# Seven quarter products instead of eight in both feed-forward products, in two passes with the activations kept in memory between them

## The chip, the cores and the metric

The kernel runs on one core of a Trainium2 chip. The metric is the device time in microseconds of one execution, given as the median of several runs. Changes under 0.3% of it are not told from none here.

## The reference

One layer of a streaming encoder for 1024 frames of width 1024, all in float32. A mixer part (three kinds of attention and recurrence, computed in `front` and `heads`) ends in `mixed @ w_out`. What the change touches comes behind it:

```python
x = x + rmsnorm(mixed, post_mix_g[l])
h = rmsnorm(x, pre_ffn_g[l])
ff = jnp.square(jax.nn.relu(h @ w_ff1[l])) @ w_ff2[l]     # w_ff1: 1024 x 4096, w_ff2: 4096 x 1024
x = x + rmsnorm(ff, post_ffn_g[l])
```

## The kernel before

Every large product is computed in three passes: an operand is cut into a high part (a copy rounded to the matmul's type, `fp32r`) and a low part (operand minus high part), and low x high, high x low and high x high are added up in one bank of PSUM. So each operand needs one copy, mostly on ScalarE, and one subtraction, mostly on VectorE, before TensorE can use it.

The function `back` holds all that is changed. It is written as one program for each engine (SyncE issues the loads and stores, ScalarE, GpSimd, VectorE, TensorE), and the programs meet at semaphores; each engine takes its instructions in the order written. It starts with the output projection (`product(j, half)`, L1648), takes rows j of 128 frames through `residual(j)` and the normalising (`rows`, `normed_rows`), and turns them with eight transposes each (`turn(j)`, L2051) into `hH` and `hL`, the transposed activations (1024 of depth in 8 blocks, 1024 frames).

The feed-forward part runs over 8 slices of 512 hidden columns (`NE`), each in 4 blocks (`FB`) of 128. `hidden_half` (L2058) makes a block of hidden columns for 512 frames: 8 blocks of depth x 3 passes = 24 matmuls of 128x512. `second_product` (L2081) multiplies a slice with its 512 rows of `w_ff2`: 16 groups (8 tiles of frames x 2 halves of columns) of 4 x 3 = 12 matmuls. On ScalarE a hidden block goes through ReLU (L1864) and square (L1867); VectorE cuts it (L1975, L1977) into `gH` and `gL`. Weights are loaded by SyncE (L1742, L1747), copied on ScalarE (L1809, L1815) and subtracted on VectorE (L1906, L1910). The sum over slices is kept in SBUF, in `acc`, 128 x 8192: VectorE adds each group's bank to it (L1987), 128 times; GpSimd sets it to zero (L1893). Slices 0 to 6 are one loop (`Fori`) on each engine:

```python
with pe.Fori(0, NE - 1) as e:
    hidden_block(e + 1, 0)
    second_product(e)
    for i in range(1, FB):
        hidden_block(e + 1, i)
second_product(NE - 1)
```

`finish(j)` normalises the rows of `acc` while the last slice still runs; behind the last matmul come an add, a square with its sum (L1883), a root, two scaled halves (L2008), two adds (L2011) and two stores (L1794).

`front` uses GpSimd and VectorE at once, and the rows below take durations from it: GpSimd subtracts 128x256 pieces (L484) while VectorE works on 128x768 tiles (L919, L927, L931).

## Time and profile before

| | |
|---|---|
| median of 3 runs | 1529.02 us (1528.37 to 1533.39) |
| span of the profiled execution, first to last instruction | 1526.5 us |
| feed-forward part, first to last matmul | 807.48 to 1517.70 us |
| TensorE busy | 1445.1 us, 95% |
| VectorE, ScalarE, GpSimd busy | 679.8, 536.7, 308.4 us |
| moved by DMA | 124.15 MB, mean 81 GB/s |

The profiled execution has no device time of its own beside the span; the median lies 2.5 us over the span. Times of rows are microseconds from the first instruction unless marked ns. PE is TensorE's matmul, PEld its weight load, DVE VectorE, ACT ScalarE, POOL GpSimd. Matmuls overlap, and the durations in their rows hold the overlap; the distance of their starts tells their pace.

### The profile page before, as it was taken

The page shows a single profiled execution, that of the slowest core. Times are in us where ns is not written, and L with a number is a line of the kernel's source. Part 1 is how long each engine was busy: PE and PEld are TensorE (multiplying, and loading weights), DVE is VectorE, ACT ScalarE, POOL GpSimd, SP SyncE. Part 2 cuts the span into 40 slices and gives each one's busy share as a digit, 9 for nine tenths or more (in the row PEclk, how much of TensorE's full clock was granted, in tenths as well). Part 3 has the DMA queues.
Part 4 walks back from the last instruction along what each step waited for, and adds up shares of the span by engine and source line. Part 5 has one row for each costly group of instructions (what it writes and reads, how often), then busy time and mean ns, then how long its engine had stood idle before and what let it go on. Part 6 is the DMA issues. An engine that isn't in the chain of part 4 may idle for free.

```text
span 1526.5 us, 27877 instructions
## 1 busy us (share of the span) xinstructions
PE 1445.1 (95%) x11404; PEld 1135.9 (74%) x11404; DVE 679.8 (45%) x1101; ACT 536.7 (35%) x1045; POOL 308.4 (20%) x423
## 2 busy tenths in 40 slices
PE   6999989989898999889999999999999999999997
PEld 5887677777676666465777888888888888888876
DVE  6244252556554375755555233242423324242347
ACT  4533231434323588875434213030211304031222
POOL 6674635423240142433001000000000000000000
PEclk9999999999999799999999999999999999999999
DMA  6554423423234603021623203020110302021024
GB/s 192 146 157 126 133 57 104 120 60 99 59 78 95 177 3 84 3 88 54 204 102 119 70 10 101 0 87 22 56 54 14 96 0 96 14 69 41 27 67 168
DMA packets 144429, 124.15 MB, mean 81 GB/s; under 512 B 31437, under 2 KB 122762, under 8 KB 144330
## 3 DMA queue, kind: packets, MB, share of 16 engines
q1 hardware_dynamic: 98044, 92.90, 20.0%
q10 hardware_dynamic: 46286, 29.84, 7.0%
q8 instruction: 73, 1.20, 0.3%
q14 instruction: 26, 0.21, 0.0%
HBM read 97.88 MB, written 24.84 MB: 80 GB/s over the span
## 4 chain that ended last, share of the span: by engine, by line
PE 48%; DVE 2%; ACT 1%; DMA 1%; issue 1%; POOLq 0%; SPq 0%; DVEq 0%; ACTq 0%
PE all_ps_b L2081 23%; PE all_ps_b L2058 22%; PE all_ps_b L1648 2%; DMA bk_acc<-in_w_out 1%; POOLq L1668 0%; DVE bk_acc L1935 0%; PE all_ps_b L2051 0%; ACT bk_acc L1836 0%; DVE bk_acc L1945 0%; DVE bk_w1L L1906 0%; DVE bk_acc L1931 0%; DVE all_hL L1951 0%; DVE all_gL L1977 0%; ACT bk_rect L1867 0%; DVE bk_acc L2008 0%
## 5 line engine op out<-in xcount | busy, mean ns | idle before, releaser
L1987 DVE TENSOR_TENSOR bk_acc<-bk_acc,all_ps_b 128x512 f32<-128x512 f32 x128 | 88.0, 687 | 275.9 <-PE all_ps_b L2081 275.8
L2058 PE MATMUL all_ps_b<-all_hH,bk_w1L 128*128 128x512 f32 x512 | 200.1, 391 | 5.1 <-PE all_ps_b L2081 2.2
L2081 PE MATMUL all_ps_b<-bk_w2H,all_gL 128*128 128x512 f32 x512 | 200.0, 391 | 2.5 <-DVE all_gL L1977 2.5
L2081 PE MATMUL all_ps_b<-bk_w2H,all_gH 128*128 128x512 f32 x512 | 199.8, 390 | 0.0
L2081 PE MATMUL all_ps_b<-bk_w2L,all_gH 128*128 128x512 f32 x512 | 199.7, 390 | 0.0
L2058 PE MATMUL all_ps_b<-all_hH,bk_w1H 128*128 128x512 f32 x512 | 199.3, 389 | 0.0
L2058 PE MATMUL all_ps_b<-all_hL,bk_w1H 128*128 128x512 f32 x512 | 199.2, 389 | 0.0
L484 POOL TENSOR_TENSOR fr_wL<-fr_raw,fr_wH 128x256 fp32r<-128x256 f32 (+1 forms) x208 | 162.7, 814 | 78.0 <-PE fr_ps_F L1259 54.5
L1259 PE MATMUL fr_ps_F<-fr_hL,fr_wH 128*128 128x512 f32 (+1 forms) x416 | 168.1, 404 | 2.6 <-DVE fr_hL L803 2.1
L1259 PE MATMUL fr_ps_F<-fr_hH,fr_wH 128*128 128x512 f32 (+1 forms) x416 | 166.1, 399 | 0.0
L1815 ACT CAST bk_w2H<-all_raw 128x1024 fp32r<-128x1024 f32 x32 | 32.9, 1047 | 355.6 <-PEq L2086 351.7
L2058 PEld LDWEIGHTS all_ps_b<-all_hH,bk_w1L 128*128 128x128 f32 x512 | 96.1, 188 | 28.3 <-issue 6.8
L2081 PEld LDWEIGHTS all_ps_b<-bk_w2H,all_gL 128*128 128x128 f32 x512 | 96.5, 188 | 23.0 <-DVE all_gL L1977 2.9
L1259 PE MATMUL fr_ps_F<-fr_hH,fr_wL 128*128 128x512 f32 (+1 forms) x416 | 112.4, 400 | 0.0
L2081 PEld LDWEIGHTS all_ps_b<-bk_w2H,all_gH 128*128 128x128 f32 x512 | 96.5, 188 | 20.2
L2081 PEld LDWEIGHTS all_ps_b<-bk_w2L,all_gH 128*128 128x128 f32 x512 | 96.5, 189 | 19.9
L2058 PEld LDWEIGHTS all_ps_b<-all_hH,bk_w1H 128*128 128x128 f32 x512 | 96.1, 188 | 20.1
L2058 PEld LDWEIGHTS all_ps_b<-all_hL,bk_w1H 128*128 128x128 f32 x512 | 96.1, 188 | 19.5
L1259 PEld LDWEIGHTS fr_ps_F<-fr_hL,fr_wH 128*128 128x128 f32 (+1 forms) x416 | 76.8, 185 | 22.4 <-issue 3.8
L1975 DVE CAST all_gH<-bk_rect 128x512 fp32r<-128x512 f32 x64 | 27.3, 427 | 145.9 <-ACT bk_rect L1867 145.9
L1259 PEld LDWEIGHTS fr_ps_F<-fr_hH,fr_wH 128*128 128x128 f32 (+1 forms) x416 | 76.9, 185 | 18.6 <-issue 2.0
L1259 PEld LDWEIGHTS fr_ps_F<-fr_hH,fr_wL 128*128 128x128 f32 (+1 forms) x416 | 75.6, 185 | 19.8 <-issue 3.2
(354 smaller groups left out, 2260.9 us busy)
## 6 DMA issues: line engine op xcount, KB each, us to landing
fr_raw<-in_w_in ACTq DMA_DIRECT2D x37, 512.0 KB, 4.2
bk_raw<-in_w_ff SPq DMA_DIRECT2D x32, 512.0 KB, 4.3
all_raw<-in_w_ff SPq DMA_DIRECT2D x32, 512.0 KB, 4.7
projected<-fr_stage ACTq DMA_DIRECT2D x39, 256.0 KB, 4.4
fr_raw<-in_w_in SPq DMA_DIRECT2D x13, 512.0 KB, 4.2
fr_xt<-in_x SPq DMA_DIRECT2D x8, 512.0 KB, 4.9
bk_acc<-in_x SPq DMA_DIRECT2D x8, 512.0 KB, 3.4
x_after_mixers<-bk_acc SPq DMA_DIRECT2D x8, 512.0 KB, 2.6
```

The costliest lines, as they stand in the source:

```text
L484: m = pool.tensor_tensor(wL[b][:, k:k + 2, 0:wd], raw[b][:, k:k + 2, 0:wd], wH[b][:, k:k + 2, 0:wd].bitcast(F32), ALU.subtract)
L1259: m = pe.matmul(F[b][0:wd, :], w[b][:, k, 0:wd], a[:, k, :], start=(at_ == 0), stop=(at_ == len(passes) - 1))
L1648: i = pe.matmul(bank[:], m[:, k, ts], w[:, k, :], start=(k == first and q == 0), stop=(k == last and q == 2), skip_group_check=True)
L1815: act.copy(w2H[:, i, :], raw2[i % 2][:]).then_inc(w2_high, 1)
L1975: dve.tensor_copy(gH[:, i, hs], g32).then_inc(g_high, 1)
L1987: dve.tensor_tensor(acc[:, j, ds], acc[:, j, ds], ybank[g % 4][:], ALU.add).then_inc(collected, 1)
L2058: m = pe.matmul(bank[s][h][:], w[s][:, k, :], a[:, k, hs], start=(k == 0 and q == 0), stop=(k == KB - 1 and q == 2))
L2081: m = pe.matmul(ybank[g % 4][:], a[:, i, ts], w[:, i, ds], start=(i == 0 and q == 0), stop=(i == FB - 1 and q == 2))
```

## The change

Both products are split into quarters, one level of Strassen's scheme in the form with seven products and shared sums. In the first one the hidden columns are taken in 16 pairs p of blocks (block p and block 16 + p), and the depth and the frames are halved. For each pair there are seven products P1 to P7 of 4 blocks of depth x 3 passes = 12 matmuls (`hidden(q)`, in the order `SEQ`; the first pairs' P1 and P2 are drawn ahead). GpSimd makes four sums of weight quarters for each pair, and GpSimd and VectorE make four sums of activation quarters once, tile by tile as they are turned. VectorE adds the products up (`drain`), rectifies and squares three quarters of the result, ScalarE the fourth (`take_c11`), and SyncE stores all to a new tensor in memory, `rectified`, 4096 x 1024.

The second product starts when the first is done. It runs over s = 0, 1, 2 (two of the seven products each: M3 and the one beside it, M1 and M2, M7 and M4) and k = 0 to 15 (128 hidden columns of either half each): 2 products x 4 tiles of frames x 3 passes = 24 matmuls for each k, added up over k in eight banks. The seventh product (`last_product`) is added behind them, tile by tile; for k under 12 (`KEPT`) its operands are prepared in s = 2 and kept in SBUF. Each quarter is loaded again for each s (`load_unit`; the two quarters of s = 0 stay for s = 1) into nine slots; `POOL_SUMS` and `DVE_SUMS` are added on GpSimd and VectorE; ScalarE copies the high parts, VectorE subtracts the low parts, into a ring `R` of four products. Between the s VectorE and ScalarE take the banks out and combine them (`take_tiles`, `tile_sum`). `acc`, its memset and the 128 adds are gone; nothing of the part is a loop any more.

The core of the diff:

```diff
--- before.py
+++ after.py
@@ -1656,40 +1656,225 @@
...
+        SEQ = [(0, P1), (1, P1), (0, P2), (1, P2), (2, P1), (2, P2)]
+        for p in range(3):
+            SEQ += [(p, i) for i in (P6, P5, P7, P4, P3)]
+        for p in range(3, NP):
+            SEQ += [(p, i) for i in (P1, P6, P2, P5, P7, P4, P3)]
+        NQ, AT = len(SEQ), {x: q for q, x in enumerate(SEQ)}
...
+        KEPT = 12
...
+            pairs_ = {0: [("b12", "b22")], 1: [("a22", "b11"), ("b22", "b21")],
+                      2: [("a21", "a22"), ("b11", "b21")] + ([("a11", "b12")] if k < KEPT else []),
+                      3: [("a21", "a11"), ("b11", "b12")]}[s]
+            UNITS += [(s, k, names) for names in pairs_]
...
+        def products(s, k):
+            if s == 0:
+                return [("a11", "b12", 1), ("temp", "b22", -1)]
+            if s == 1:
+                return [("a11", "b11", 1), ("a12", "b21", 1)]
+            if s == 2:
+                return [("a22", "b21", 1), ("a21", "b11", -1)]
+            return [("a11", "b12", 1)]
+        POOL_SUMS = {0: [("b12", "b12", "b22", ALU.subtract), ("temp", "a11", "a12", ALU.add)],
+                     1: [("a11", "a11", "a22", ALU.add), ("b11", "b11", "b22", ALU.add), ("b21", "b21", "b22", ALU.add)],
+                     2: [("a11", "a21", "a11", ALU.subtract), ("a21", "a21", "a22", ALU.add), ("b12", "b11", "b12", ALU.add)],
+                     3: [("a11", "a21", "a11", ALU.subtract)]}
+        DVE_SUMS = {0: [], 1: [("a12", "a12", "a22", ALU.subtract)], 2: [("b21", "b21", "b11", ALU.subtract)],
+                    3: [("b12", "b11", "b12", ALU.add)]}
...
+        def LEAD(q):
+            return min(9 + 2 * (q - EARLY + 1), q + 9)
+        FIRST_F = {NQ - 6: (0,), NQ - 5: (1,), NQ - 3: (2,), NQ - 2: (3,)}
...
+            def load_unit(u):
+                s, k, names = UNITS[u]
+                if u < SLOTS:
+                    sp.wait_ge(made, NQ - SLOTS + u + 1)
+                else:
+                    sp.wait_ge(*split_done(*UNITS[u - SLOTS][0:2]))
...
+            def take_c11(p):
+                m = M[p, 0]
+                c = cbuf[m % 3]
+                act.wait_ge(made, AT[p, P2] + 1)
...
+                act.activation(c, b(p, 1)[:], ACT.Relu).then_inc(c11_taken, 1)
+                act.wait_ge(c11_taken, p + 1)
+                act.activation(c, c, ACT.Square).then_inc(c11_ready, 1)
...
+            t_split(2, 45)
+            residual(TB - 1)
+            take_p1(0)
+            take_high(TB - 2)
+            rows(TB - 1)
+            t_split(3, 45)
+            t_split(4, 45)
+            take_p1(1)
+            split(4)
+            split(5)
+            take_c11(0)
+            for n in (2, 1, 3, 4):
+                t_split(n, 6)
+            take_c11(1)
+            take_high(TB - 1)
+            take_p1(2)
+            t_split(2, 7)
+            t_split(1, 7)
+            split(6)
...
+                    act.wait_ge(*used_at(at - 4))
+                raw_ready(s, k, a)
+                act.copy(R[at % 4][0], place(s, k, a)).then_inc(f_high, 1)
+                raw_ready(s, k, w)
+                if sign < 0:
+                    act.activation(R[at % 4][2], place(s, k, w), ACT.Copy, scale=-1.0).then_inc(f_high, 1)
+                else:
+                    act.copy(R[at % 4][2], place(s, k, w)).then_inc(f_high, 1)
...
+            for p in range(NP):
+                a, w = rawA[p % 3], rawB[p % 2]
+                pool.wait_ge(a_in[p % 3], 16 * (p // 3 + 1))
+                pool.wait_ge(b_in[p % 2], 16 * (p // 2 + 1))
+                if p:
+                    pool.wait_ge(low, max(AT[p - 1, P5], AT[p - 1, P6]) + 1)
+                else:
+                    pool.wait_ge(turned, 2 * TB)
+                pool.tensor_tensor(S1, w[:, LO], w[:, HI], ALU.add).then_inc(ssum, 1)
+                pool.wait_ge(ssum, 4 * p + 1)
+                pool.tensor_tensor(S2, S1, a[:, LO], ALU.subtract).then_inc(ssum, 1)
+                pool.tensor_tensor(w[:, LO], a[:, LO], w[:, LO], ALU.subtract).then_inc(ssum, 1)
+                pool.wait_ge(ssum, 4 * p + 2)
+                if p:
+                    pool.wait_ge(low, AT[p - 1, P3] + 1)
+                pool.tensor_tensor(S4, a[:, HI], S2, ALU.subtract).then_inc(ssum, 1)
+            for s, k in BLOCKS:
+                for n, (to, a, w, op) in enumerate(sums_of(POOL_SUMS, s, k)):
+                    if n == 0:
+                        for u in units_of(s, k):
+                            pool.wait_ge(u_in[unit_slot(u)], IN_COUNT[u])
+                        if s == 1:
+                            pool.wait_ge(*split_done(0, k))
+                    if to == "temp":
+                        if k < 2:
+                            pool.wait_ge(u3_made, NP - 1 + k)
+                        else:
+                            pool.wait_ge(*split_done(0, k - 2))
+                    if (s, to) == (2, "a21") and k < KEPT:
+                        pool.wait_ge(f_sum, POOL_AT[s, k, "a11"])
+                    pool.tensor_tensor(place(s, k, to), place(s, k, a), place(s, k, w), op).then_inc(f_sum, 1)
...
+                if i == P6:
+                    dve.wait_ge(p1_taken, p + 1)
+                    if p:
+                        dve.wait_ge(c12_sum, p)
+                    else:
+                        dve.wait_ge(t_low, len(T_ORDER))
+                    dve.tensor_tensor(u2, p1_of(p), b(p, 2)[:], ALU.add).then_inc(u2_made, 1)
+                if i == P7:
+                    if p:
+                        dve.wait_ge(c21_sum, p)
+                    dve.tensor_tensor(u3, p1_of(p), b(p, 2)[:], ALU.add).then_inc(u3_made, 1)
+                    c = room(p, 3)
+                    dve.wait_ge(u3_made, p + 1)
+                    dve.tensor_tensor(c, u3, b(p, 3)[:], ALU.add).then_inc(c22_sum, 1)
+                    dve.wait_ge(c22_sum, p + 1)
+                    rectify(p, 3)
...
+            for s, k in BLOCKS:
+                add_pieces(s, k)
+                for n in range(len(products(s, k))):
+                    if number(s, k, n) >= 4:
+                        split_product(s, k, n)
+                    if (s, k, n) == (1, 0, 1):
+                        for j in range(4):
+                            dve.wait_ge(m3_taken, j + 1)
+                            tile_sum(j, 5 + j, c12[j], c22[j], bankB[j][:], ALU.subtract, c12_made)
+                    if (s, k, n) == (2, 0, 1):
+                        for j in range(4):
+                            dve.wait_ge(m1_taken, j + 1)
+                            tile_sum(j, 9 + j, c22[j], c22[j], bankA[j][:], ALU.add, m1_added)
+                        for j in range(4):
+                            tile_sum(j, 13 + j, c11[j], c11[j], bankB[j][:], ALU.add, m7_added)
...
+                for k in range(QB):
+                    for n, (w, a) in enumerate(((wL, aH), (wH, aL), (wH, aH))):
+                        m = pe.matmul(bank[:], w[:, k, :], a[:, k, :], start=(begins and k == 0 and n == 0),
+                                      stop=(k == QB - 1 and n == 2), skip_group_check=True)
+                m.then_inc(made, 1)
...
+            def second_product(s, k, n):
+                at = number(s, k, n)
+                pe.wait_ge(f_low, at + 1)
...
+                    if s == 1 and k == 0:
+                        if n:
+                            pe.wait_ge(c12_made, j + 1)
+                        else:
+                            pe.wait_ge(m3_taken, j + 1)
+                    if s == 2 and k == 0:
+                        if n:
+                            pe.wait_ge(m7_added, j + 1)
+                        else:
+                            pe.wait_ge(m1_taken, j + 1)
+                            pe.wait_ge(m1_added, j + 1)
+                    m = tile((bankB if n else bankA)[j], j, R[at % 4], begins, last)
+                    if last:
+                        m.then_inc(tile_done, 1)
+                if not last:
+                    m.then_inc(used, 1)
...
+            def last_product(j, ks):
+                for k in ks:
+                    if k < KEPT:
+                        pe.wait_ge(k_low, 2 * k + 2)
+                        pieces = m6[k]
+                    else:
+                        pe.wait_ge(f_low, number(3, k, 0) + 1)
+                        pieces = R[number(3, k, 0) % 4]
+                    if k == 0:
+                        pe.wait_ge(c21_made, j + 1)
+                    m = tile(bankB[j], j, pieces, False, k == NK - 1)
+                if ks[-1] == NK - 1:
+                    m.then_inc(tile_done, 1)
...
+            hidden(0)
             turn(TB - 2)
-            pe.wait_ge(w1_low[1], 2)
-            hidden_half(1, 0)
+            for q in (1, 2, 3):
+                hidden(q)
             turn(TB - 1)
-            pe.wait_ge(freed, TB)
-            pe.wait_ge(hlow, 2 * TB)
-            hidden_half(0, 1).then_inc(hidden[0], 1)
-            hidden_half(1, 1).then_inc(hidden[1], 1)
-            hidden_block(0, 2)
-            hidden_block(0, 3)
-            with pe.Fori(0, NE - 1) as e:
-                hidden_block(e + 1, 0)
-                second_product(e)
-                for i in range(1, FB):
-                    hidden_block(e + 1, i)
-            second_product(NE - 1)
+            for q in range(4, NQ):
+                hidden(q)
+            for s in range(3):
+                for k in range(NK):
+                    for n in range(2):
+                        second_product(s, k, n)
+            for j in range(2):
+                last_product(j, range(KEPT))
+            for j in range(2):
+                last_product(j, range(KEPT, NK))
+            for j in range(2, 4):
+                last_product(j, range(NK))
...
+    rect_d = nc.dram_tensor("rectified", [DFF, T], F32, kind="Internal").ap()
```

## Rows read from the trace of the kernel before

**Rows 1.** The page, 40 slices of the span: TensorE's busy share and granted clock, in tenths.
```profile
PE   6999989989898999889999999999999999999997
...
PEclk9999999999999799999999999999999999999999
```
**Rows 2.** Stretches of the span: length, busy us (instructions) of PE, PEld, DVE, ACT, POOL, clock, DMA.
```profile
807.48:1517.70 710.22, 702.60 (x3089) 578.57 (x3087) 257.99 (x365) 156.95 (x236) 6.95 (x1) 1.00 0.18 58
1517.70:1526.50 8.80, 0.00 (x0) 0.00 (x0) 3.87 (x8) 1.50 (x5) 0.00 (x0) 0.78 0.31 120
```
**Rows 3.** The page, groups by line: form and count, busy us, mean ns, idle before.
```profile
L1987 DVE TENSOR_TENSOR bk_acc<-bk_acc,all_ps_b 128x512 f32<-128x512 f32 x128 | 88.0, 687 | 275.9 <-PE all_ps_b L2081 275.8
L2058 PE MATMUL all_ps_b<-all_hH,bk_w1L 128*128 128x512 f32 x512 | 200.1, 391 | 5.1 <-PE all_ps_b L2081 2.2
```
**Rows 4.** Timeline of PE inside a loop turn: start, us, instruction; 27 intervals.
```profile
1239.86 0.39 PE L2081 MATMUL all_ps_b<-bk_w2H,all_gH 128*128 128x512 f32 x1
...
1245.98 0.39 PE L2081 MATMUL all_ps_b<-bk_w2H,all_gH 128*128 128x512 f32 x1
```
**Rows 5.** Waits of PE from 800 us on: who for whom, total us, times, longest.
```profile
PE all_ps_b L2081 <- DVE all_gL L1977: 2.5, 1, 2.5
PE all_ps_b L2058 <- PE all_ps_b L2081: 2.2, 7, 0.3
PE all_ps_b L2058 <- DVE all_hL L1951: 1.7, 1, 1.7
PE all_ps_b L2058 <- DVE bk_w1L L1906: 1.3, 1, 1.3
```
**Rows 6.** Timeline of PE: a turn of tiles, a loop turn, behind the last wait.
```profile
819.26 1.04 PE L2051 MATMUL all_ps_b<-all_ident,bk_acc 128*128 128x128 f32 x8
...
910.47 0.39 PE L2081 MATMUL all_ps_b<-bk_w2H,all_gH 128*128 128x512 f32 x1
911.15 0.47 PE L2058 MATMUL all_ps_b<-all_hH,bk_w1L 128*128 128x512 f32 x1 [0.30 <-PE all_ps_b L2081]
...
1475.65 0.63 PE L2081 MATMUL all_ps_b<-bk_w2L,all_gH 128*128 128x512 f32 x1
1476.08 0.63 PE L2081 MATMUL all_ps_b<-bk_w2H,all_gH 128*128 128x512 f32 x1
...
1478.50 0.39 PE L2081 MATMUL all_ps_b<-bk_w2H,all_gH 128*128 128x512 f32 x1
```
**Rows 7.** Groups by line and form, 700 to 800 us: operations of 128x512.
```profile
L1915 DVE TENSOR_TENSOR bk_w2L<-bk_acc,bk_w2H 128x512 fp32r<-128x512 f32 x8 | 5.4, 692 | 14.4 <-ACT bk_w2H L1819 14.4
...
L1843 ACT CAST all_hH<-all_ps_b 128x512 fp32r<-128x512 f32 x10 | 5.3, 583 | 0.1
...
L1819 ACT CAST bk_w2H<-bk_acc 128x512 fp32r<-128x512 f32 x8 | 5.0, 622 | 15.3 <-DMA bk_acc<-in_w_out 15.2
```
**Rows 8.** GpSimd: timeline at 70 to 115 us, then a group by line and form.
```profile
70.00 2.82 POOL L484 TENSOR_TENSOR fr_wL<-fr_raw,fr_wH 128x256 fp32r<-128x256 f32 x4
...
102.93 5.57 POOL L484 TENSOR_TENSOR fr_wL<-fr_raw,fr_wH 128x256 fp32r<-128x256 f32 x4
...
114.36 1.03 POOL L478 CAST fr_wH<-fr_raw 128x1024 fp32r<-128x1024 f32 x1
...
L484 POOL TENSOR_TENSOR fr_wL<-fr_raw,fr_wH 128x32 fp32r<-128x32 f32 x8 | 1.8, 252 | 8.0 <-PE fr_ps_F L1259 8.0
```
**Rows 9.** Timeline of VectorE in the same time.
```profile
101.00 0.96 DVE L919 TENSOR_TENSOR fr_bt<-fr_kk,fr_sa 128x768 f32<-128x768 f32 x1
...
103.59 1.49 DVE L927 SCALAR_TENSOR_TENSOR fr_at<-fr_kk,fr_at 128x768 f32<-128x768 f32 x1
105.00 1.49 DVE L931 SCALAR_TENSOR_TENSOR fr_sw<-fr_sw,fr_ks 128x768 f32<-128x768 f32 x1
...
114.33 0.69 DVE L956 TENSOR_TENSOR fr_bonus<-fr_vs,fr_ps_S 128x512 f32<-128x512 f32 x1 [1.88 <-PE fr_ps_S L1319]
```
**Rows 10.** A stretch: length, PE busy, granted clock, DMA share, GB/s.
```profile
820.00:860.00 40.00, 37.03 (x164) 1.00 0.37 120
```

More of the change, by code:

```diff
@@ L1874, in _ @@
[L1874 to L1886 removed]
+            t_split(1, 45)
@@ new lines, in _, with take_tiles @@
+            for q in range(EARLY, NQ):
+                p, i = SEQ[q]
+                if i == P1:
+                    take_p1(p)
+                if i == P2:
+                    take_c11(p)
+                while next_q < min(NQ, LEAD(q)):
+                    split(next_q)
+                    next_q += 1
+                for n in FIRST_F.get(q, ()):
+                    split_product(0, n // 2, n % 2)
+            def take_tiles(to, bank, after, done):
+                for j in range(4):
+                    act.wait_ge(tile_done, after + j + 1)
+                    act.copy(to[j], bank[j][:]).then_inc(done, 1)
@@ new lines, in _ @@
+            t_split(1, 45)
+            t_split(2, 45)
+            residual(TB - 1)
+            take_low(TB - 2)
+            normed_rows(TB - 1)
+            t_split(3, 45)
+            t_split(4, 45)
+            split(4)
+            split(5)
+            for n in (2, 1, 3, 4):
+                t_split(n, 6)
+            take_low(TB - 1)
+            t_sums()
+            t_split(2, 7)
+            t_split(1, 7)
+            split(6)
+            t_split(3, 7)
+            t_split(4, 7)
+            split(7)
@@ new lines, in split_kept @@
+            def split_kept(k):
+                aH, aL, wH, wL = m6[k]
+                dve.wait_ge(k_high, 2 * k + 1)
+                dve.tensor_tensor(aL, place(2, k, "a11"), f32(aH), ALU.subtract).then_inc(k_low, 1)
+                dve.wait_ge(k_high, 2 * k + 2)
+                dve.tensor_tensor(wL, place(2, k, "b12"), f32(wH), ALU.subtract).then_inc(k_low, 1)
+            for q in range(EARLY, NQ):
+                drain(q)
+                while next_q < min(NQ, LEAD(q)):
+                    split(next_q)
+                    next_q += 1
+                for n in FIRST_F.get(q, ()):
+                    split_product(0, n // 2, n % 2)
```

819 lines of the change are left out of this document (574 added, 245 removed).

## The prediction

> **What bounds the kernel now.** I read the slices of the page first: from the middle of the span on, TensorE shows 9 tenths or more in every slice, and its clock is granted in full nearly throughout [rows 1]. The table of stretches cuts out the two feed-forward products: from the first matmul of L2058 at 807.48 us to the end of the last of L2081 at 1517.70 us, 710.2 us, with TensorE busy 702.6, VectorE 258.0, ScalarE 157.0, GpSimd 7.0; behind it 8.8 us of tail [rows 2]. The groups by line say that this is 3072 matmuls of 128x512, all alike, and that VectorE mostly waits for them (275.9 us before its adds at L1987) [rows 3]. A row gives 0.39 us for a matmul, but they overlap; what one costs is the distance of starts: 27 of them in 1239.86 to 1245.98, 6.12 us, 0.2267 us each [rows 4]. 3072 x 0.2267 = 696.4 us; two groups of eight transposes are 2.1; so 11.7 us are waits. The list of waits and the starts name them: 7 loop turns (0.68 us between the starts across a turn instead of 0.23 and a little more at the next one, some 0.54 each, 3.8 in all), about 3.4 us at the entrance (1.7 and 1.3 and what goes with them), and 4.3 us in the last slice (2.5 of waiting, then about nine matmuls at up to 0.43 instead of 0.23), where there is nothing to fill with [rows 5, 6]. So TensorE is the bound here, and 98% of the stretch is matmuls.
>
> **What goes.** 1536 + 1536 matmuls become 16 x 7 x 4 x 3 = 1344 for the first product (16 pairs of column blocks, 7 products, 4 blocks of depth, 3 passes for high and low parts) and 16 x 7 x 4 x 3 = 1344 for the second. 384 fewer of the same shape: 384 x 0.2267 = **87.1 us**. The code is no longer a loop: 3.8 us less. The last slice's wait and the slow matmuls after it go: 4.3. The two waits at the entrance are replaced by others, counted below: 3.4. The memset of 7 us on GpSimd goes, too; it only lay beside. Sum of what goes: 98.6 us.
>
> **The new entrance.** Six products (first quarter operands only) can run before the sums of quarters of the activations are there: 72 matmuls and two turns, 16.3 + 2.1 us after 807.5, so TensorE is at product seven (P6) at 826. ScalarE has to do in that time, one after the other: two squares with their sums and a root (1.8), take_p1 three times, take_high of tiles 6 and 7 at three copies each, four split copies of 128x512 for tile 6, two for tile 7, three weight splits, two rows of 1024 (the square with its root, and two splits of 1024: 3.5) and c11 twice (2.4). At 0.58 to 0.62 us for a 512-column copy [rows 7] that is about 19 us, starting 0.8 us late behind t_split(2,45). It ends near 827.5; on VectorE come three quarter sums of the last tile (1.9) and the low parts (0.6 each) in the same chain, so P6 starts near 830 to 831. I take 5 us of waiting, 1.5 for the slow clock after it and 1.5 for the first pairs, where VectorE has two splits a product to make up its lead: **8 us**, bounds 0 (all hidden) and 15 (each step also queued behind GpSimd).
>
> **Pass one.** A pair lasts 84 x 0.2267 = 19.0 us. VectorE has 7 splits, 5 adds from PSUM, 3 rectifies: 15 x 0.6 to 0.69, about 10 us; ScalarE 10 operations of 0.6, 6 us; GpSimd 4 sums, 5 us; splits lead by up to nine products. All of it lies beside the matmuls: 0. Between the passes TensorE waits for the last drain of P3, 0.2 + 0.69 plus a semaphore: **1.2 us**. The stores to memory have 0.85 us of issue and some 3 us of flight a block; the first blocks read back after the last product (k = 2, 3) have 11 us until they are due.
>
> **Pass two: where the next bound is.** One k is 24 matmuls, 5.44 us. Per k there are: s=0: 2 GpSimd sums, 4 VectorE operations; s=1: 3 and 5; s=2, k under 12: 3 and 7 (one sum, four low parts, two kept ones); ScalarE 4 to 6 copies, 3.7 us at most. All are 128x512 with both inputs in SBUF. Alone, VectorE takes 0.69 us for one, about 0.61 from start to start [rows 7]. For GpSimd the trace has no 128x512 sum; four of 128x256 take 2.82 us alone, 0.705 each, and one of 128x32 0.25 [rows 8]: 2.0 ns a column, so 1.22 us for 512 (bounds: 0.87 by half that slope, 1.41 by twice the 256-column one). By these s=2 would be 7 x 0.61 = 4.3 us on VectorE and 3 x 1.22 = 3.7 on GpSimd, and both would fit beside 5.44.
>
> But they don't run beside each other. From 102.93 us on the same four GpSimd subtractions take 5.57 us, 1.39 each, exactly while VectorE runs operations with two SBUF inputs, and these, of 768 columns, start every 1.41 us, where one alone takes 0.96 and about 0.87 from start to start [rows 8, 9]. 1.41 for a pair whose parts alone are 0.705 + 0.87 = 1.58: the two engines take turns, at 0.89 of the sum. Where VectorE reads PSUM (0.69 us at 114.33) GpSimd's cast beside it stays at 1.03 [rows 8, 9]. The Trainium skill (GPSIMD Engine Reference, Key points) says that GpSimd shares its SBUF interfaces with VectorE and that instructions with two SBUF inputs contend; by that rule, too, the two columns add up. The same page (Elementwise, side-by-side cycle accounting) has 4497 ns for 2048 columns, so an estimate of 1.12 us for 512; no run here shows that shape, and with it the sum below would be about 5 us less.
>
> So per k: s=0: (4 x 0.61 + 2 x 1.22) x 0.89 = 4.3 us, under 5.44; s=1: (5 x 0.61 + 3 x 1.22) x 0.89 = 6.0; s=2: (7 x 0.61 + 3 x 1.22) x 0.89 = 7.1. TensorE then waits 0.53 us a k in s=1, from about k=4 on, when VectorE's lead of up to four products is eaten: 12 x 0.53 = 6. In s=2 1.62 a k over 11: 18. Between s=1 and s=2 TensorE's first tiles wait for m1_added, which VectorE reaches only behind both splits of k=0 (5 operations and GpSimd's 3 between them, 6 us, against 2.7 of matmuls), and then four m7 adds stand ahead of the next split: 4 + 2 = 6. Sum **30 us**. Between s=0 and s=1 the copy and c12 have 2.7 us of matmuls over them: 0. Behind k=12 of s=2 it is (5 x 0.61 + 1.22) x 0.89 = 3.8, no wait; the last product needs nothing new for 12 of 16 k. Bounds of this term: 0 (the leads and nine load slots cover it) and 60 (bubbles of 1 us a k on top, since sum, copy and low part go over three engines).
>
> DMA: s=2 loads 6 x 256 KB, 1.57 MB a k, 289 GB/s at full pace, 223 at 7.1 us. One stretch of the same queue moved 120 GB/s at a share of 0.37, so full use would be about 324 [rows 10]: it carries it, and I take 0; a share of 0.9 is the closest rival for the blame.
>
> The tail has the same chain as before behind its last matmul (add, square, root, two scaled halves, two stores): 0.
>
> **Sum.** 1526.5 - 98.6 + 8 + 1.2 + 30 = 1467.1 us of span. The median of the runs is 1529.0, 2.5 over this span, and I keep that: **1470 us**.
>
> **The rivals.** (a) The sharing doesn't bite: the load slots let GpSimd run up to four k ahead, and its sums fall into VectorE's pauses. Then 1467 - 30 = 1437, so 1440 us. For it: s=0 has slack, and VectorE stands idle for several us ahead of each block of tile sums. Against: GpSimd takes its turn whenever a slot is free, so its lead is never spent. 25%. (b) The chain over the engines binds on top of the shared reads: sum on VectorE or GpSimd, copy on ScalarE, low part on VectorE, each with 0.1 to 0.3 us between; 1 us more for each of 28 k, 1498 us. 12%. (c) The slower side: the many short waits of s=1 and s=2 bring TensorE's clock to its lower level and keep it there. After the wait of 2.5 us the starts went from 0.23 to 0.43 us for a while (1475.65 to 1476.08), 1.2 GHz in place of 2.4; after the one of 1.7 us at 820 there is no such stretch [rows 5, 6]. At that level a k takes 24 x 0.427 = 10.2 us, against 6.0 and 7.1: over all 28 k 100 us more, 1570 us, slower than before; it decides from about 17 k at that level on. Against it: with 10.2 us a k nobody has to be waited for, the matmuls are dense again, and after the wait at 1471 the clock came back once they were (0.39 us for the matmul at 1478.50, 0.63 for those before) [rows 6]. The Trainium skill (TensorE: Matmul & The Clock Gate, A second HAM failure mode) has a kernel that idles a little between groups of matmuls and swings between the two levels; by that rule some of (c) would come. 6%. That the change doesn't do what it says would show as more than 2688 matmuls; the loops of the diff leave no room for that.
>
> **How the numbers follow.** Forecast 57%, (a) 25, (b) 12, (c) 6. The likeliest's own range is 1453 to 1488. Of the 20% left out at most, (c)'s bulk and the ends of (a) and (b) are part: 1437 to 1500. A difference under 0.3%, 4.6 us, can't be told from none here. (c) in part only could land anywhere between, so slower is 6%, same 1%, faster 93%.
>
> **What would show it.** After: 2688 matmuls of 128x512 in the feed-forward part, 0.2267 us apart in pass one, in a stretch near 310 + 8 us. In pass two, s=0 dense; from s=1 on gaps before products, released by VectorE's splits; VectorE's 128x512 subtractions and GpSimd's sums there well above 0.69 and 1.22 us, VectorE and GpSimd together busy nearly all the time. If the sums stay at 1.22 and TensorE has no gaps, (a) is right. If VectorE idles while TensorE waits, (b), or DMA if the releaser is a landing. I am wrong altogether if pass one has waits on each pair, or if the granted clock is under 0.95 over pass two.

## The result, and the profile after

| | before | after |
|---|---|---|
| median, same chip | 1531.2 us (4 runs) | 1483.49 us (4 runs, 1480.28 to 1488.01) |
| ratio | | 0.9687 (95%: 0.9663 to 0.9710) |
| span; device time of the profiled execution | 1526.5 | 1482.4; 1484.15 us |
| feed-forward part, first matmul to end of last | 710.2 us | 811.04 to 1473.84: 662.8 us |
| TensorE, VectorE, GpSimd busy | 1445.1, 679.8, 308.4 us | 1373.6, 925.7, 610.1 us |
| moved by DMA | 124.15 MB | 185.34 MB |

3.1% faster. The forecast was 1470 us, 13.5 under the result, which lies inside the likeliest case's own range, 1453 to 1488. The measure that I use below is the *excess* of a stretch: its length less 0.2268 us for each of its matmuls, the pitch of [rows 4] taken over the dense stretches. Before, the part had 710.2 - 3072 x 0.2268 = 13.5 us of it; after, 662.8 - 2688 x 0.2268 = 53.2.

The slices of the page after, for TensorE, its clock and VectorE; the second product is the last nine or so. Where [rows 1] had nines, there are now eights, and it is VectorE that has the nines:
```profile
PE   6999989989899899898989799999999999998897
...
DVE  6244162565652465667375985555556989999985
...
PEclk9999999999999799999999999999999999999999
```
The table of stretches, columns as in [rows 2]: the entrance, pass one, then s = 0, s = 1, s = 2 (k under 12, k from 12 on), the last product, the tail:
```profile
807.00:862.00 55.00, 44.73 (x193) 35.66 (x192) 46.97 (x55) 28.86 (x53) 32.43 (x20) 0.94 0.28 88
862.00:1130.90 268.90, 268.90 (x1187) 222.44 (x1186) 146.78 (x216) 78.94 (x137) 77.82 (x56) 1.00 0.37 116
1133.40:1220.30 86.90, 86.90 (x383) 71.93 (x384) 72.37 (x60) 35.91 (x64) 61.32 (x39) 1.00 0.61 215
1220.30:1320.00 99.70, 92.90 (x387) 70.65 (x386) 99.61 (x89) 39.12 (x73) 71.38 (x44) 1.00 0.53 174
1320.00:1402.00 82.00, 67.13 (x265) 50.94 (x266) 81.24 (x83) 34.16 (x64) 49.99 (x32) 0.96 0.61 197
1402.00:1430.00 28.00, 27.29 (x120) 22.12 (x119) 27.74 (x36) 14.77 (x28) 10.49 (x7) 1.00 0.87 291
1430.00:1473.70 43.70, 43.66 (x192) 35.96 (x192) 28.02 (x50) 12.42 (x32) 0.00 (x0) 1.00 0.37 143
1473.70:1482.40 8.70, 0.14 (x1) 0.00 (x0) 3.81 (x7) 0.93 (x3) 0.00 (x0) 0.72 0.16 61
```
Pass one is dense. In s = 1 VectorE is busy 99.6 of 99.7 us, in s = 2 81.2 of 82: it is the bound there, and 1 - 67.13/82 = 18% of TensorE's time is lost. By the starts of the 2688 matmuls the excess is 13.4 us at the entrance (to 854.40), 4.1 in pass one with its end, 0.7 in s = 0, 11.7 in s = 1, 22.1 in s = 2 below k = 12, 0.9 above, 0.1 in the last product: 53.0 (the last matmul's end is the other 0.2). TensorE's waits from 807 us on, who for whom, total, times, longest:
```profile
PE all_ps_b L2661 <- DVE ro_w1A L2492: 10.1, 9, 2.7
PE all_ps_b L2661 <- DVE ro_hH L2492: 8.2, 8, 4.3
PE all_ps_b L2652 <- DVE ro_slot L2336: 7.9, 3, 5.6
PE all_ps_b L2661 <- DVE pl_raw L2466: 2.3, 1, 2.3
PE all_ps_b L2652 <- ACT pl_p L2141: 1.6, 1, 1.6
...
PE all_ps_b L2652 <- ACT pl_raw L2141: 0.8, 1, 0.8
```
The first four are VectorE: two rows for the low parts of the second product, one for the entrance, one for the border of the passes. The two of ScalarE are its copies of P1 out of PSUM at the entrance. No landing releases TensorE. For VectorE the list of waits has no row in s = 1 and in s = 2 below k = 12, while GpSimd waits 41.2 us for landings there: a late sum of GpSimd is not what holds VectorE up.

The timelines of VectorE (first fence) and GpSimd (second) around the largest gap of the second product, and TensorE's rows there (third):
```profile
1334.37 0.68 DVE L2499 TENSOR_TENSOR ro_gL<-pl_slot,ro_gL 128x512 fp32r<-128x512 f32 x1
1334.97 1.77 DVE L2480 TENSOR_TENSOR pl_slot<-pl_slot 128x512 f32<-128x512 f32 x1
1336.67 1.78 DVE L2487 TENSOR_TENSOR ro_w1A<-pl_slot,ro_w1A 128x512 fp32r<-128x512 f32 x1
...
1346.86 1.74 DVE L2480 TENSOR_TENSOR pl_slot<-pl_slot 128x512 f32<-128x512 f32 x1
```
```profile
1334.44 5.16 POOL L2329 TENSOR_TENSOR pl_slot<-pl_slot 128x512 f32<-128x512 f32 x3 [9.31 <-DMA pl_slot<-in_w_ff]
...
1344.65 1.73 POOL L2329 TENSOR_TENSOR pl_slot<-pl_hT,pl_slot 128x512 f32<-128x512 f32 x1
```
```profile
1344.65 2.01 PE L2661 MATMUL all_ps_b<-ro_xt 128*128 128x512 f32 x8
1350.94 2.62 PE L2661 MATMUL all_ps_b<-ro_hH 128*128 128x512 f32 x6 [4.28 <-DVE ro_hH L2492]
```
The operation before 1334.97, with GpSimd idle, lasts 0.68 us and the next starts 0.60 after it. From there eight in a row start 1.70 us apart (1334.97 to 1346.86 is 7 x 1.70): as soon as GpSimd has work, the engines alternate, one instruction each. GpSimd's sums beside VectorE (first row) and alone (second), from the entrance of the same trace:
```profile
830.99 1.74 POOL L2313 TENSOR_TENSOR all_sb_masks<-pl_w1A,pl_y 128x512 f32<-128x512 f32 x1
840.84 1.28 POOL L2306 TENSOR_TENSOR pl_y<-pl_xt 128x512 f32<-128x512 f32 x1 [8.11 <-DVE ro_slot L2336]
```
So a pair takes 1.70 us where the parts alone are 0.60 + 1.28 = 1.88: 0.90 of the sum. Over all of s = 1, 41 of VectorE's 81 such operations last over 1.5 us, for 42 GpSimd sums; in s = 2 below k = 12 it is 30 of 83, for 32 sums. **Each GpSimd sum lengthens one VectorE operation by 1.10 us.** Behind the 4.3 us wait about nine matmuls follow at the lower level of the clock (starts 0.43 us apart, 2.62 us for six; the granted clock is 0.58 from 1350.9 to 1355 us). One more such stretch stands behind the wait of 2.2 us at 1371.59; the two cost 3.5 us. In s = 1 there is none, at a granted clock of 1.00; there the first start behind a wait comes 0.34 us later instead of 0.23, 2.3 us in all.

### The profile page after: what moved, and what is told of

Its sections match the earlier page's. It is cut to its first block and busy times, and to the rows that moved or that the text cites. A ratio compares the mean times of both kernels' runs of the same rounds, so it can differ in the third digit from the quotient of the medians.

```text
span 1482.4 us, 27708 instructions
## 1 busy us (share of the span) xinstructions
PE 1373.6 (93%) x11020; PEld 1066.3 (72%) x11020; DVE 925.7 (62%) x1319; ACT 627.7 (42%) x1265; POOL 610.1 (41%) x622
## 2 busy tenths in 40 slices
DMA packets 182906, 185.34 MB, mean 125 GB/s; under 512 B 35709, under 2 KB 127034, under 8 KB 182778
## 5 line engine op out<-in xcount | busy, mean ns | idle before, releaser
L2329 POOL TENSOR_TENSOR pl_slot<-pl_slot 128x512 f32<-128x512 f32 x51 | 84.1, 1658 | 45.1 <-DMA pl_slot<-in_w_ff 31.6
L2652 PE MATMUL all_ps_b<-ro_hH,ro_slot 128*128 128x512 f32 x272 | 88.4, 391 | 3.2 <-ACT pl_p L2141 1.6
L2661 PE MATMUL all_ps_b<-ro_hH 128*128 128x512 f32 x312 | 79.3, 401 | 10.5 <-DVE ro_hH L2492 8.2
L2661 PE MATMUL all_ps_b<-ro_w1A 128*128 128x512 f32 x300 | 75.8, 401 | 10.1 <-DVE ro_w1A L2492 10.1
L2661 PEld LDWEIGHTS all_ps_b<-ro_hH 128*128 128x128 f32 x312 | 58.7, 191 | 27.5 <-DVE ro_hH L2492 12.4
L2661 PE MATMUL all_ps_b<-ro_hL 128*128 128x512 f32 x312 | 76.8, 392 | 1.8 <-DVE ro_hL L2492 1.1
L2661 PEld LDWEIGHTS all_ps_b<-ro_w1A 128*128 128x128 f32 x300 | 56.5, 192 | 26.4 <-DVE ro_w1A L2492 14.8
L2661 PE MATMUL all_ps_b<-ro_xt 128*128 128x512 f32 x300 | 73.1, 391 | 1.5 <-DVE ro_xt L2490 0.8
L2661 PEld LDWEIGHTS all_ps_b<-ro_hL 128*128 128x128 f32 x312 | 58.0, 188 | 16.5 <-DVE ro_hL L2492 2.4
L2661 PEld LDWEIGHTS all_ps_b<-ro_xt 128*128 128x128 f32 x300 | 56.0, 188 | 14.8 <-DVE ro_xt L2490 1.6
```

The lines of the kernel that those rows point to most:

```text
L2329: pool.tensor_tensor(place(s, k, to), place(s, k, a), place(s, k, w), op).then_inc(f_sum, 1)
L2652: m = pe.matmul(bank[:], w[:, k, :], a[:, k, :], start=(begins and k == 0 and n == 0), stop=(k == QB - 1 and n == 2), skip_group_check=True)
L2661: m = pe.matmul(bank[:], a[:, ts], w, start=(begins and n == 0), stop=(ends and n == 2), skip_group_check=True)
```

## The experiments

Before's median beside the first four was 1532.42 us (7 runs), beside e5 to e8 1530.14 (9), e9 1531.28 (9), e10 1532.83 (9).

**e1: all sums of s = 1, 2, 3 on VectorE, one block ahead** (shown without the waits that go with them).
```diff
-  1: [("a11", ...), ("b11", ...), ("b21", ...)], 2: [("a11", ...), ("a21", ...), ("b12", ...)], 3: [("a11", ...)]   # POOL_SUMS
+  1: [], 2: [], 3: []                                                # the same sums now stand in DVE_SUMS
-                add_pieces(s, k)
+                if ORDER[s, k] + 1 < len(BLOCKS):
+                    add_pieces(*BLOCKS[ORDER[s, k] + 1])
```


> Pass two, s = 1, 2 and 3: GpSimd's sums are moved to VectorE, each one k ahead of its split; s = 0 and pass one stay. Theory 'turns' (two-input instructions of VectorE and GpSimd exclude each other, so a GpSimd sum costs VectorE's queue 1.1 us where VectorE's own costs 0.6): per k s=1 takes 8 x 0.6 = 4.8 us, under the 5.44 of the matmuls, and s=2 10 x 0.6 = 6.1; the 34.7 us over the matmuls' own time in s=1 and s=2 fall to about 10 to 14, so 20 to 25 us less, near 1460 us. Rival 'chain' (the way sum, copy, low part over three engines is too long, not the shared reads): VectorE's queue gets 2 or 3 operations longer per k and nothing is shortened, so no gain or a few us slower. Rival 'landings' (GpSimd waits for loads, 55 us in all by the trace): the loads wait for the same slots, so no change.

Measured: 1472.32 us (4 runs), ratio 0.9611 (0.9582 to 0.9641). The excess of s = 1 is gone (11.7 to 0.0), with three more operations a block on VectorE. That of s = 2 stayed: 22.1 to 21.6. The stretch 1310 to 1390 us and VectorE's waits in s = 2:
```profile
1310.00:1390.00 80.00, 67.01 (x259) 52.38 (x258) 67.96 (x111) 37.17 (x67) 0.00 (x0) 0.91 0.65 202
```
```profile
DVE pl_slot L2486 <- DMA pl_slot<-in_w_ff: 4.4, 3, 2.1
DVE pl_hT L2486 <- DMA pl_slot<-in_w_ff: 3.8, 3, 1.8
DVE pl_slot L2486 <- DMA pl_hT<-in_w_ff: 2.5, 3, 2.0
```
VectorE is no longer full (68 of 80 us); it waits 10.7 us for landings. The nine slots hold three blocks of s = 2, and with the sums one block ahead a load had one block's time from free slot to use. A new cause, made by my edit; e6 tests it.

**e2: GpSimd's sums in the second product replaced by a fill** (the sums are left out).
```diff
-  pool.tensor_tensor(place(s, k, to), place(s, k, a), place(s, k, w), op).then_inc(f_sum, 1)
+  pool.memset(place(s, k, to), 0.5).then_inc(f_sum, 1)
```


> Each GpSimd sum of pass two is replaced by filling its destination with 0.5 (the sums are left out, so the output is not the reference's); all waits and signals stay. A fill reads nothing and takes about 0.6 us instead of 1.3 alone. 'Turns': VectorE's 128x512 subtractions are back at 0.69 us throughout, the excess of s=1 and s=2 falls from 34.7 to about 3 to 6 us (tile sums at the borders): 1453 us or so. 'Chain': only 0.7 us a sum are saved, at most 5 us in all. 'Landings': unchanged, 1483.

Measured: 1448.13 us (2 runs), ratio 0.9457 (0.9420 to 0.9494). The whole excess of the second product is gone, 35.5 to 0.0. VectorE, GpSimd and the stretch of s = 2 in it:
```profile
1331.50 0.68 DVE L2499 TENSOR_TENSOR ro_wo<-pl_slot,ro_wo 128x512 fp32r<-128x512 f32 x1
```
```profile
1330.96 1.58 POOL L2329 MEMSET pl_slot<- 128x512 f32 x3 [2.55 <-DMA pl_slot<-in_w_ff]
```
```profile
1307.00:1372.40 65.40, 65.40 (x291) 54.14 (x290) 55.83 (x90) 40.16 (x71) 15.84 (x31) 1.00 0.89 292
```
Beside the three fills VectorE's operation stays at 0.68 us (the pitch at 0.60), and DMA carries s = 2 at full pace at a share of 0.89: neither the chain over the engines nor the loads bound the changed kernel. The fill also takes less of GpSimd's own time (0.53 us for 1.28), so by itself this run doesn't tell sharing from GpSimd's own lateness. What does is that VectorE waits for no sum in s = 1 and s = 2 of the changed kernel, the count of slow operations, s = 1 of e1, and a row of e5.

**e3: loads of s = 1, 2, 3 with half the columns** (the other half is not loaded).
```diff
+                    n = HALF // 2 if s else HALF
-                    sp.dma_start(piece(s, k, name), src[...,  at:at + HALF]).then_inc(got, 16)
+                    sp.dma_start(piece(s, k, name)[:, 0:n], src[..., at:at + n]).then_inc(got, 16)
```


> The quarters loaded for s = 1, 2, 3 bring only their first 256 of 512 columns (half of the operand is left over from before, so the output is not the reference's); number of loads, waits and signals stay. 'Landings' as a matter of bandwidth: the excess of s=1 and s=2 (34.7 us) falls by more than half. 'Turns': it stays within 4 us of 34.7, since 1.57 MB for a k fit into 5.44 us at the rate that the trace after shows (291 GB/s).

Measured: 1488.81 us (2 runs), ratio 0.9723 (0.9681 to 0.9764). The stretches of s = 1 and s = 2:
```profile
1226.30:1326.30 100.00, 91.29 (x385) 72.51 (x385) 97.16 (x88) 37.08 (x68) 81.02 (x43) 0.98 0.29 90
1326.30:1408.00 81.70, 65.18 (x261) 50.59 (x262) 81.44 (x84) 36.47 (x69) 49.74 (x31) 0.96 0.35 102
```
Half the traffic (90 and 102 GB/s for 174 and 197), the same excess: 13.0 and 22.6 us. Bandwidth is not the cause.

**e4: the first pair's four weight sums on VectorE.**
```diff
+            dve.tensor_tensor(S1, w[:, LO], w[:, HI], ALU.add).then_inc(ssum, 1)          # and S2, ahead of t_split(2, 7)
+            dve.tensor_tensor(w[:, LO], a[:, LO], w[:, LO], ALU.subtract).then_inc(ssum, 1)   # and S4, ahead of split(6)
-            for p in range(NP):          # GpSimd
+            for p in range(1, NP):
```


> At the entrance, the four weight sums of pair 0 go from GpSimd to VectorE, behind the sums of the last tile. In the trace after GpSimd makes them from 825.98 to 832.7 us and VectorE's splits beside them take 1.77 us instead of 0.69; TensorE then waits 5.75 us for P6. 'Turns': VectorE is quicker by about 6 us there and pays 2.4 for the sums, so the wait falls to about 2 us and the slow clock behind it (1.9 us) goes: 5 us less, 1478. Rival (ScalarE's queue sets the entrance, as the prediction had it): VectorE gets 2.4 us more to do, so 0 to 2 us slower.

Measured: 1484.65 us (4 runs), ratio 0.9692 (0.9662 to 0.9722): a miss. TensorE's row behind the longest wait:
```profile
841.34 2.08 PE L2662 MATMUL all_ps_b<-ro_gL,ro_slot 128*128 128x512 f32 x4 [3.69 <-DVE ro_slot L2336]
```
That wait fell from 5.6 to 3.7 us, the entrance's excess from 13.4 to 11.3; the other waits stood. Four turns of 1.10 us went and 4 x 0.60 us of work came into VectorE's chain, 2.0 us on balance, which is what was gained; the expectation had put the turns at 6 us. VectorE's two operations of 1024 columns ahead of them still lasted 2.30 and 2.31 us, beside the quarter sums of a turned tile on GpSimd. The slow matmuls behind the wait stayed, too. 2 us can't be seen in these medians.

**e5: a copy of one input in place of GpSimd's sum in the second product** (the second input is left out).
```diff
-  pool.tensor_tensor(place(s, k, to), place(s, k, a), place(s, k, w), op).then_inc(f_sum, 1)
+  pool.tensor_copy(place(s, k, to), place(s, k, a)).then_inc(f_sum, 1)
```


> GpSimd's sums in the second product are replaced by a copy of one of their inputs (same place, same waits, one input instead of two); the values are therefore not the reference's. Theory A (the two engines give way to each other only where both instructions read two operands from SBUF): beside a copy VectorE's 128x512 operations keep their 0.60 us pitch, the excess of the second product (35 us in the changed kernel, 0 with a fill in place of the sum) goes to under 3 us and the time to 1447 to 1452. Theory B (any GpSimd instruction that reads from SBUF takes its turn with VectorE): the pitch stays at 1.7 us for as long as GpSimd has work, a copy may be somewhat shorter than a sum, and the time is 1470 to 1484.

Measured: 1450.96 us (4 runs), ratio 0.9481 (0.9449 to 0.9513); excess of the second product 0. The time is theory A's, the rows are not:
```profile
1329.85 1.09 DVE L2497 TENSOR_TENSOR ro_wo<-pl_hT,ro_wo 128x512 fp32r<-128x512 f32 x1
1330.87 1.09 DVE L2499 TENSOR_TENSOR ro_wo<-pl_hT,ro_wo 128x512 fp32r<-128x512 f32 x1
1331.88 0.68 DVE L2480 TENSOR_TENSOR pl_hT<-pl_hT 128x512 f32<-128x512 f32 x1
```
```profile
1330.35 1.07 POOL L2329 COPY pl_slot<-pl_hT 128x512 f32<-128x512 f32 x1
```
```profile
1185.96 0.62 POOL L2329 COPY pl_slot<-pl_slot 128x512 f32<-128x512 f32 x1
```
Beside a copy VectorE's operations start 1.02 us apart: a GpSimd instruction with one SBUF input takes its turn, too, and costs VectorE 0.42 us for the sum's 1.10. With three turns a block, 7 x 0.60 + 3 x 0.42 = 5.5 us, just TensorE's 5.44. The last row is a copy with VectorE idle: at 0.62 us it is little longer than e2's fill (0.53), which costs VectorE nothing. So it is the read that makes the turn; and of the two that read, each costs about 0.2 us less than its own length alone (0.62 and 1.28).

**e6: as e1, but in s = 2 and 3 the sums in their own block.**
```diff
+                if s < 2 and (s, k) != (1, NK - 1):
+                    add_pieces(*BLOCKS[ORDER[s, k] + 1])
+                if s >= 2:
+                    add_pieces(s, k)
```


> As the first experiment (all sums of slices one to three on VectorE), but in slices two and three VectorE makes a block's sums right ahead of that block's splits and not one block earlier, so that a load has one block (about 6 us) more to land. Theory A (what was left of the loss in slice two, 21.6 us, is the wait for landings: the slots of a block came free only two blocks before its sums were wanted, and its six loads of 256 KB need most of one block's time): slice two loses 12 blocks x (10 x 0.60 - 5.44) = 7 us and a few for the eight adds at its border, 5 to 11 in all, and the time falls from 1472 to 1458 to 1463. Theory B (VectorE's own work and the border set it, landings only fill its idle time): slice two still loses 18 to 22 us, the time stays at 1470 to 1474. With the sums in their own block ScalarE's copies wait for them; if that chain binds, slice two gets worse than 21.6 and the time is over 1474.

Measured: 1458.44 us (4 runs), ratio 0.9537 (0.9499 to 0.9576). VectorE has no wait for a landing in s = 2; its excess is 9.3 us. TensorE there:
```profile
1327.12 3.02 PE L2670 MATMUL all_ps_b<-ro_w1A 128*128 128x512 f32 x12 [0.51 <-DVE ro_w1A L2498]
...
1333.37 0.96 PE L2670 MATMUL all_ps_b<-ro_hH 128*128 128x512 f32 x3 [0.51 <-DVE ro_hH L2498]
```
The same wait at every k, 6.25 us apart: VectorE's ten operations with their gaps (10 x 0.60 and 0.2 of waiting within the sums), 0.80 over TensorE's 5.44. Only the order of the sums differs from e1, so of e1's 21.6 us the landings were 12.3.

**e7: fills for GpSimd's sums in the first product** (they are left out).
```diff
-  pool.tensor_tensor(S1, w[:, LO], w[:, HI], ALU.add).then_inc(ssum, 1)
+  pool.memset(S1, 0.5).then_inc(ssum, 1)                       # and S2, w[:, LO], S4, and the four quarter sums of each tile
```


> GpSimd's sums in the first product (quarter sums of the turned activations, and the weights' sums of all pairs) are replaced by fills with a constant; values are not the reference's, the second product is as in the changed kernel. Theory A (about half of the 13.4 us lost at the entrance is VectorE kept waiting by GpSimd's two-input sums): the entrance loses 5 to 8 us, the gap of 5.98 us ahead of the seventh product is under 2.5. Theory B (the entrance is the chain residual, turn, copy, quarter sum, split, on which both engines lie one after the other, and sharing costs little): 11 to 13 us stay. The rest of pass one is unchanged at about 4 us by both, since only one operation in two falls beside a sum there and TensorE's operands are two products ahead.

Measured: one time of 1484.49 us, which says little, since its feed-forward part began at 818.32 us. Within the trace the entrance's excess is 4.65 us for 13.4, and the longest wait this:
```profile
839.17 1.19 PE L2648 MATMUL all_ps_b<-ro_gL,ro_slot 128*128 128x512 f32 x4 [1.47 <-DVE ro_slot L2332]
```
8.8 us less, a little more than theory A wanted; a fill shortens GpSimd's own part of the chain as well, so how much of the 8.8 is sharing is open. The rest of pass one stayed (3.6 us).

**e8: e6 and e4 together** (both diffs).

> The order of e6 and, in addition, the four weight sums of the first pair on VectorE (they took 2 us off the gap ahead of the seventh product when tried alone). If the two act in different stretches, their gains add: e6's time less about 2 us, 1456 to 1461, some 24 us faster than the changed kernel and 70 faster than the kernel before. If e6's order brings nothing, 1469 to 1472.

Measured: 1458.40 us (5 runs), ratio 0.9533 (0.9506 to 0.9560). The entrance's excess fell to 11.4 as in e4, but the median shows nothing of it against e6: 2 us are under what differs from execution to execution ahead of the part (below).

**e9: e8 with the four short blocks of s = 2 at k = 1, 5, 9, 13.**
```diff
+        FREE = [1, 5, 9, 13]
+        HELD = [k for k in range(NK) if k not in FREE]
-        BLOCKS = ... + [(3, k) for k in range(KEPT, NK)]
+        BLOCKS = ... + [(3, k) for k in FREE]
-                if s == 2 and k < KEPT:
+                if s == 2 and k in HELD:
```


> As e8, with the four blocks of slice two that have only six VectorE operations (the others have ten: their sixth product's operands are made there and set aside) at k = 1, 5, 9, 13 instead of 12 to 15. Theory A (slice two of e6 and e8 loses what VectorE needs beyond TensorE's 5.44 us a block: its pitch there is 6.25 us, 0.80 too much in each of twelve blocks = 9.6, measured 9.34): a short block gives back 5.44 - 6 x 0.61 = 1.8 us of lead, three long ones in a row take 2.4, so some 0.6 us are lost after each group and 2 to 4 in all, 5 to 7 us less than e8: 1451 to 1454. Theory B (the wait at every k of slice two in e8 is a chain of landing, sum, copy and low part that lasts as long in any block, and the lead does not build up in a short block): each of the twelve long blocks still loses 0.8, the time stays at 1457 to 1460.

Measured: 1459.80 us (5 runs), ratio 0.9531 (0.9518 to 0.9544). Neither theory's total: the twelve waits went (excess of s = 2 below k = 12: 9.3 to 2.1), as A says, but one of 4.8 us came at the end of s = 2, with nine slow matmuls behind it. VectorE and TensorE there:
```profile
1396.80 2.48 DVE L2531 TENSOR_TENSOR pl_hH<-pl_hH,all_ps_b 128x512 f32<-128x512 f32 x4
1399.19 2.47 DVE L2531 TENSOR_TENSOR pl_hL<-pl_hL,all_ps_b 128x512 f32<-128x512 f32 x4
```
```profile
1400.02 2.61 PE L2684 MATMUL all_ps_b<-ro_gH 128*128 128x512 f32 x6 [4.77 <-DVE pl_hL L2531]
```
The short blocks had stood at the end, and their spare time had covered the second block of s = 3 and the adds of c11, which go ahead of c21's. The last product waits for c21 alone.

**e10: e9, with c21's adds first, right behind the first block of s = 3.**
```diff
-                    if (s, k) == (3, FREE[1]):
+                    if (s, k) == (3, FREE[0]):            # VectorE and ScalarE
+                            tile_sum(j, 21 + j, c21[j], c21[j], bankB[j][:], ALU.subtract, c21_made)   # now ahead of c11's
```


> As e9, and at the end of slice two VectorE and ScalarE take the tiles of M4 and make the sums of c21 right after the first block of slice three (c21 first, then c11) instead of after the second block and after the four sums of c11. In e9 the last products wait 4.9 us for the first c21 tile: 4 operations of block two and 4 sums of c11, 8 x 0.60 = 4.8 us, stand ahead of it on VectorE, since no lead is left there. Theory A (these eight operations are that wait): it falls to 0 to 1 us, slice two loses 2 to 3.5 us in all where e9 lost 7.2 and e8 9.3, the nine slow matmuls behind it (1.7 us) go, and the time is 1451 to 1454. Theory B (the tile itself, its copy on ScalarE or the end of TensorE's own accumulation is what is late): the wait stays over 3 us and the time at 1457 to 1460.

Measured: **1451.97 us** (5 runs, 1449.22 to 1454.06), ratio 0.9472 (0.9459 to 0.9485), the best version. The end of s = 2 has no wait:
```profile
1395.23 2.88 PE L2684 MATMUL all_ps_b<-ro_xt 128*128 128x512 f32 x12
1397.95 1.54 PE L2684 MATMUL all_ps_b<-ro_gH 128*128 128x512 f32 x6
```
The second product loses 3.7 us where the changed kernel lost 35.5; s = 1 has TensorE busy all 87.0 us, s = 2 (1308.6 to 1376) 66.4 of 67.4.

## Why the prediction was right or wrong

The span came out 15.3 us over the 1467.1 of the sum; the median, 1.1 us over the span where I had kept 2.5, is 13.5 over the forecast. The parts of the span (the prediction counted the 2.1 us of transposes neither in what goes nor in the entrance, so they are taken out of both measures here):

| step | predicted | measured | difference |
|---|---|---|---|
| what goes | -98.6 | -87.1 - (13.5 - 2.1) = -98.5 | +0.1 |
| entrance | +8 | 13.4 - 2.1 = +11.3 | +3.3 |
| pass one, end of it | 0 + 1.2 | 1.7 + 2.4 | +2.9 |
| second product | +30 | +35.5 | +5.5 |
| ahead of the part | 0 | +3.6 | +3.6 |

**TensorE's pitch and the count of matmuls** held: 2688 at 0.2268 us, dense in pass one.

**The second product.** The forecast's mechanism was the right one, and (a) and (b) fall: e2 takes away the reads and all of the excess goes, e5 grades it, e3 takes the bandwidth out. A pair measured at 0.90 of the sum of its parts, where 0.89 was read from shapes that were only relatives [rows 8, 9]; GpSimd's sum was estimated at 1.22 us and is 1.28.

The term that was mis-sized is s = 1, 6 us against 11.7. The step that failed is the length of a block: the formula took 0.89 of all eight operations, but only the three pairs overlap, and the two operations of VectorE that have no partner cost their full 0.60. With the measured prices a block is 5 x 0.60 + 3 x 1.10 = 6.30 us, not 6.0, and the first thirteen blocks of s = 1 do start 6.30 us apart (6.50 the first): 0.86 us a block for the 0.53 forecast. The smaller part is the lead. I let it cover the first four blocks, and it covered none: GpSimd ran twelve sums of s = 1 from 1202.3 to 1222.2 us, beside VectorE's last work of s = 0, and at the border four adds from PSUM, 2.47 us in a row, stand ahead of the next split.

s = 2 with its border was put at 24 and is 23.1, and that is partly luck. A block with three turns is 7 x 0.60 + 3 x 1.10 = 7.50 us there (k = 7 to 9 measure that), not 7.1; for the 1.62 us a block forecast it makes 2.06, and over 11 blocks 4.8 us more. But while GpSimd waits for landings VectorE works alone (from 1325.6 to 1335.0 us, for one), and only 30 of the 36 turns due fell into the stretch, 6.6 us less. With 1.12 us in place of 1.22 for GpSimd's sum the forecast would have fallen by 0.27 us a block, some 6 us and not 5; the measured 1.28 lies on the other side.

The Trainium skill (SBUF — State Buffer, Who interferes with whom) says that a VectorE instruction with two SBUF inputs contends with a GpSimd one that reads SBUF, not with one that only writes, and that the shared port pair is an exclusive lock. The trace, e2 and e5 agree in kind (1.70, 0.60 and 1.02 us a start); what each turn costs stands only in the rows.

**The entrance.** The failing step is ScalarE's 19 us as what ends last ahead of P6. ScalarE stood idle for 6.1 us; VectorE was late, since GpSimd's sums for the last tiles and the first pair fell on its chain. VectorE, ScalarE and TensorE in the changed kernel:
```profile
823.57 2.32 DVE L2381 TENSOR_TENSOR ro_wo<-pl_hT,ro_wo 128x1024 fp32r<-128x1024 f32 x1
825.81 2.38 DVE L2336 TENSOR_TENSOR ro_slot<-pl_y,ro_slot 128x512 fp32r<-128x512 f32 x2
828.11 1.77 DVE L2381 TENSOR_TENSOR ro_gL<-pl_hL,ro_gL 128x512 fp32r<-128x512 f32 x1
...
831.50 1.77 DVE L2381 TENSOR_TENSOR ro_wo<-pl_hH,ro_wo 128x512 fp32r<-128x512 f32 x1
```
```profile
836.31 0.62 ACT L2133 CAST ro_gL<-pl_hL 128x512 fp32r<-128x512 f32 x1 [6.13 <-DVE pl_hL L2391]
```
```profile
832.94 0.39 PE L2652 MATMUL all_ps_b<-ro_hH,ro_slot 128*128 128x512 f32 x1
838.91 4.09 PE L2652 MATMUL all_ps_b<-ro_gL,ro_slot 128*128 128x512 f32 x9 [5.59 <-DVE ro_slot L2336]
```
From 821 to 833 us two operations of 1024 columns (the one shown and one at 821.35) last 1.0 us longer than alone (one alone takes 1.29 in e4's trace), four of 512 columns 1.1 each (one of them in the row of two): 6.4 us. P6 came at 838.9, not at 830 to 831. I had priced the sharing in the second product and not here; it was only in the bound of 15, which held. The nine matmuls in 4.09 us are the slow stretch behind the wait; such matmuls cost 1.9 us at the entrance in all, 1.5 foreseen. By starts P6 waits 5.75 us, 5 foreseen, although both it and TensorE's arrival were late: 3.7 us more are lost ahead of P6, where the sum had nothing, most of it in the two waits for ScalarE's copies (1.8 and 0.9 us by starts) and behind the second turn. The 1.5 us for the first pairs came later and are the 1.7 of pass one.

**Pass one** had no steady waits. A second one of 1.7 us came at 859.6, when the second pair's operands were late from the same chain. The border cost 2.4 us instead of 1.2: the last product ends at 1131.1, but two splits for the second product (1131.38 and 1131.98) stand ahead of its add in VectorE's order, which starts at 1132.59.

**Ahead of the part.** Its first matmul came 3.6 us later. Most of it lies in code that neither kernel changes: the output projection begins at 707.05 in the trace of before, at 709.80 in that of after, and at 707.9 to 715.3 in those of the experiments.
```profile
709.80 0.50 PE L1648 MATMUL all_ps_b<-all_gH,all_hL 128*128 128x512 f32 x1
```
That is why stretches are compared here, and why 2 us at the entrance could not be seen in medians.

**DMA 0 and tail 0** held, and (c) didn't come: shares of 0.53 to 0.87 without a wait of TensorE for a landing, 8.6 us of tail, a granted clock of 0.96 in s = 2. The lower level appeared behind three waits only, those of 5.6, 4.3 and 2.2 us, for some nine matmuls each (1.9 us at the entrance, 3.5 in s = 2); behind those of 2.25 us at 1133.37 and 2.7 us at 1328.30, and behind all the short ones of s = 1, it did not. The sign that VectorE and GpSimd are both busy nearly all the time held for VectorE alone: GpSimd has 71.4 of 99.7 us in s = 1 and 50.0 of 82 in s = 2.

## What to carry to other kernels

An elementwise operation with two SBUF inputs moved to GpSimd is not free for VectorE: here it cost VectorE 1.10 us a turn, where doing it itself costs 0.60, so on a full VectorE the offload loses even before its own length counts. Price a shared resource in every stretch where both users meet, the entrance too, and by the pair: an operation without a partner gets no discount. Count the lead of a pipeline as zero behind a border at which the same engine must first drain results, or ahead of which the next stage's sums already take their turns. And when one bound is lifted, place the operations with time to spare next to those that have none, and look at what stood behind the old slack: e9 moved a wait, e10 removed it.
